# Forgetting attention followed by a gated recurrent block: GpSimd splits one turned chunk of four rows in each head

## The chip, the cores and the metric

One NeuronCore of a Trainium2 chip runs the whole two-layer trunk in one launch. The metric is the device time of the launch in microseconds; lower is better. "SyncE" is the engine that only issues transfers.

## The reference, cut to what matters

x is (1, 2048, 1024) in float32. Layer 0 is forgetting attention over 16 heads of width 64; layer 1 is a gated linear recurrence (RG-LRU). Each layer ends in `LayerNorm(alpha * x + sublayer(x))`. The change touches only the core of the attention:

```python
for blk in range(S // Q_BLOCK):                      # 16 rows of 128 queries
    s = einsum("bhqd,bhkd->bhqk", q[.., q0:q1], k[.., :q1])
    s = s + cum[.., q0:q1, None] - cum[.., None, :q1]
    p = softmax(where(causal, s, -inf))
    outs.append(einsum("bhqk,bhkd->bhqd", p, v[.., :q1]))
...
return (o * silu(gate)) @ w_out
```

## The kernel before, in words

The kernel has four stages: the projection of the attention (`project`), the attention (`attend`), then the output projection, norm and second projection, and the recurrence (`recur`). Each engine runs its own program and they meet only through semaphores, so an instruction that waits holds up everything behind it on its engine. `attend` takes from about 751 to 1600 us.

To keep float32 accuracy on the fast matmul path, a factor is split in a rounded high part and a low part that is the rest (value minus high part); a product is then made from the parts.

**Work units.** A *row* is 128 queries of one head against all keys up to them; a head has 16 rows (0 to 15), and row i has i+1 blocks of 128 keys, in *chunks* of up to 4 blocks (512 keys): i//4+1 chunks. Two heads make a *pair* (8 pairs), so a pair has 32 rows and 80 chunks. Each pair is 32 *steps*, one for each row, and the engines work on different rows in one step s:

- **TensorE** scores row s, chunk by chunk (L779, L780), turns (transposes) row s-3 chunk by chunk into one of four PSUM buffers (`turn`, L793), and in between weighs the values with a *group* of two rows (`weigh`, L813: the high and the low part of the turned probabilities against the values). The group of rows 2g and 2g+1 is weighed in steps 2g+5 and 2g+6, and its first product comes after the first four scores and turns of its step. So rows 8 and 9 are first needed in step 13, rows 10 and 11 in step 15.
- **VectorE** takes the scores of row s out of PSUM into `probs` with a running minimum (L945 for the last chunk of a row, L948 for the others) and makes the low part of row s-3's chunks out of PSUM (`low`, L956).
- **ScalarE** makes the high part of row s-3's chunks out of PSUM (`high`, L879), then the exponential of row s-1 (L869), and in every odd step moves the finished group out of PSUM (`move`, L894 and L895).
- **GpSimd** runs a loop over the 128 groups: `add_halves(n)` (L738, after ScalarE's move), then `finish(n - 4)`: multiply the gate by the softmax scale (L746, which waits until the gate and the scale are loaded), two multiplications with the attention (L752 to the rounded high part, L753 unrounded), one subtraction for the low part (L755). L755 marks the result as ready.
- **SyncE** stores that result (`store_y`, L693), loads gates two groups ahead (L674) and, once in each head, loads the whole next head (`load_head`, L666 and L667: six pieces of 512 KB, two small ones, and values of 1 MB). All of this stands in one queue in program order. In the loop over n, gate n+2 comes first, then the store of result n, then the head's load, when n+5 is a multiple of 8. So `load_head` stands behind the store of the results n = 3, 11, 19, ..., and the gates n = 6, 14, 22, ... stand directly behind it:

```python
for n in range(ALL):
    if n + 2 < ALL - LAG + 2:
        load_gate(n + 2)
    ...
    store_y(n)
    ...
    ahead = n + LAG + 1
    if ahead % GROUPS == 0 and ahead < ALL:
        load_head(ahead // GROUPS, 1)
    if ahead % GROUPS == GT and ahead // GROUPS + 1 < PAIRS:
        load_head(ahead // GROUPS + 1, 0)
```

Here ALL is 128, LAG 4, GROUPS 16, GT 8 and PAIRS 8: 7 heads are loaded by the first of the two conditions inside the stage, 7 by the second. A turn waits until VectorE has made the low part of the chunk that had the buffer before (L788). A weighing waits until the low parts of both its rows are made (L806).

The functions that the diff touches:

Of the kernel before, what the change touches and what calls it, by code (L numbers as in the profile page):

```python
# [19 lines left out]
P = 128  # L20
BANK = 512
ALU = mybir.AluOpType
ACT = mybir.ActivationFunctionType
# [31 lines left out]
def raw(ap):  # L55

    return ap.bitcast(F32)
# [431 lines left out]
def wait(engine, sem, value):  # L489

    if not isinstance(value, int) or value > 0:
        engine.wait_ge(sem, value)
# [7 lines left out]
def attend(nc, stage, qs, ks, vs, gs, cum, ys):  # L500
# [11 lines left out]
    S = qs.shape[2]  # L512
    D = qs.shape[1]
    QT = S // P
    GT = QT // 2
    GW = 2 * P
    STEPS = 2 * QT
# [20 lines left out]
    def width(s, j):  # L538
        return min(BANK, (s % QT + 1) * P - j * BANK)

    with ExitStack() as ctx:
        a = Alloc(nc, ctx, stage)
        q1, q2, k1, k2, val, probs, ph, pl = ({} for _ in range(8))
# [33 lines left out]
        yh = a.sb("yh", [HEAD_DIM, 2, GW], F32R)  # L577
        yl = a.sb("yl", [HEAD_DIM, 2, GW], F32R)
        rden_rows = a.sb("rden_rows", [2 * HG, 2, P])
        a.sb("free", [P, 5 * P])  # L580
        mask = a.sb("mask", [P, BANK])
        least = a.sb("least", [P, ROWS, PB])
        den = a.sb("den", [P, 2, 2 * HG])
# [24 lines left out]
        turned = a.sem("turned")  # L608
        high_out = a.sem("high_out")
        low_out = a.sem("low_out")  # L610
        weighed = a.sem("weighed")
        rden_ready = a.sem("rden_ready")
        rden_turned = a.sem("rden_turned")
# [5 lines left out]
        scaled = a.sem("scaled")  # L619
        gated = a.sem("gated")  # L620
        y_ready = a.sem("y_ready")
        def sync(sp, behind):

            def head_rows(h):
# [96 lines left out]
        def gpsimd(pool):  # L721
            pa_gpsimd(pool)
            pa["summed"](pool)
            nc.gpsimd.memset(mask[:, :], 0.0).then_inc(const_ready, 1)
            pool.wait_ge(const_ready, 1)
            nc.gpsimd.affine_select(out=mask[:, BANK - P:], in_=mask[:, BANK - P:], compare_op=ALU.is_ge, fill=MASKED,
                                    base=0, pattern=[[-1, P]], channel_multiplier=1).then_inc(const_ready, 1)
            pa["products"](pool)
            pool.wait_ge(const_ready, 2)
            nc.gpsimd.memset(raw(q2[1][HEAD_DIM:HEAD_DIM + 4, :]), 1.0).then_inc(ones_ready[1], 1)  # L730
            pool.wait_ge(ones_ready[1], 1)
            nc.gpsimd.memset(raw(k2[1][HEAD_DIM:HEAD_DIM + 4, :]), 1.0).then_inc(ones_ready[1], 1)
            pool.wait_ge(ones_ready[1], 2)
            pa["stored"](pool, pa["last"] + 1)

            def add_halves(n):
                pool.wait_ge(moved, 2 * n + 2)
                nc.gpsimd.tensor_tensor(att[:, n % AR, :], att[:, n % AR, :], low_sum[:, n % 2, :], ALU.add)\  # L738
                    .then_inc(summed, 1)

            def finish(n):

                b, f = n % 2, n // HG
                pool.wait_ge(gate_loaded[n % 4], 16 * (n // 4 + 1))
                pool.wait_ge(scale_loaded[f % 2], 16 * (f // 2 + 1))
                nc.gpsimd.tensor_tensor(gate[:, n % 4, :], scale[:, f % 2, n % HG, :], gate[:, n % 4, :], ALU.mult)\  # L746
                    .then_inc(scaled, 1)
                wait(pool, y_stored[b], 32 * (n // 2))
                wait(pool, scaled, n + 1)
                wait(pool, summed, n + 1)  # L750
                wait(pool, y_ready, n)
                nc.gpsimd.tensor_tensor(yh[:, b, :], att[:, n % AR, :], gate[:, n % 4, :], ALU.mult).then_inc(gated, 1)  # L752
                nc.gpsimd.tensor_tensor(y[:, :], att[:, n % AR, :], gate[:, n % 4, :], ALU.mult).then_inc(gated, 1)  # L753
                wait(pool, gated, 2 * n + 2)
                nc.gpsimd.tensor_tensor(yl[:, b, :], y[:, :], raw(yh[:, b, :]), ALU.subtract).then_inc(y_ready, 1)  # L755

            for n in range(ALL):
                add_halves(n)
                if n >= LAG:
                    finish(n - LAG)  # L760

        def tensor(pe):
# [20 lines left out]
            def turn(it, s, j):  # L783

                if j == 0:
                    wait(pe, probs_ready, it * STEPS + s + 1)
                c = first[s] + j
                wait(pe, low_out, it * CH + c - TB + 1)  # L788
                if it == 0 and c == 0:
                    pa["out"](pe)  # L790
                for k in range(width(s, j) // P):
                    t0 = (j * PB + k) * P
                    mm = nc.tensor.transpose(tps[c % TB][:, k, :], probs[s % ROWS][:, t0:t0 + P], ident[:, :])  # L793
                mm.then_inc(turned, 1)

            def weigh(it, g, lo, hi):

                hp, gh, b = g // GT, g % GT, g % 2
                KT = 2 * gh + 2
                if lo == 0:  # L800
                    if isinstance(it, int) and it == 0 and hp == 0:
                        if gh % 2 == 0:
                            pe.wait_ge(first_val[gh // 2], 16)
                    elif gh == 0:
                        wait(pe, val_loaded[hp], 16 * (it + hp))
                    wait(pe, low_out, it * CH + first[2 * g + 1] + n_chunks[2 * g + 1])  # L806
                    wait(pe, moved, 2 * (it * GROUPS + g - 1))
                    if g % HG == 0:
                        wait(pe, rden_out, (it * GROUPS + g) // HG)
                for kt in range(lo, hi):  # L810
                    c0 = P if kt == KT - 1 else 0
                    for t in (ph, pl):
                        mm = nc.tensor.matmul(ops[b][:, 0, c0:GW], val[hp][:, kt, :], t[b][:, kt, c0:GW],  # L813
                                              start=(kt == 0 and t is ph), stop=(kt == KT - 1 and t is pl))
                if hi == KT:
                    mm.then_inc(weighed, 1)
                    if g % HG == HG - 2:
                        f = (it * GROUPS + g) // HG
                        wait(pe, rden_ready, f + 1)
                        nc.tensor.transpose(ops[b][0:2 * HG, 1, 0:P], rden[:, f % 2, :], ident[:, :]).then_inc(rden_turned, 1)  # L820
# [36 lines left out]
        def scalar(act, beside):  # L857
# [15 lines left out]
            def high(it, s, j):  # L873
                i, g = s % QT, s // 2
                if j == 0:
                    wait(act, weighed, it * GROUPS + g - 1)
                c, n = first[s] + j, width(s, j) // P
                wait(act, turned, it * CH + c + 1)
                nc.scalar.activation(ph[g % 2][:, j * PB:j * PB + n, i % 2 * P:(i % 2 + 1) * P],  # L879
                                     tps[c % TB][:, 0:n, :], ACT.Copy).then_inc(high_out, 1)  # L880

            def move(it, g):
                n, b = it * GROUPS + g, g % 2
# [36 lines left out]
        def vector(dve, beside):  # L920
# [13 lines left out]
            def take(it, s, j):  # L934

                if j == 0:
                    wait(dve, turned, chunks_before(it, s - ROWS + 1))
                c, w = first[s] + j, width(s, j)
                wait(dve, scored, it * CH + c + 1)
                if j:  # L940
                    wait(dve, scores_out, it * CH + c)
                out, scores, found = probs[s % ROWS][:, j * BANK:j * BANK + w], sps[c % SB][:, 0:w], least[:, s % ROWS, j:j + 1]
                before = least[:, s % ROWS, j - 1:j] if j else None
                if j + 1 == n_chunks[s]:
                    nc.vector.tensor_tensor_reduce(out, scores, mask[:, BANK - w:], 1.0, before if j else 3 * MASKED,  # L945
                                                   ALU.add, ALU.min, found).then_inc(scores_out, 1)
                else:
                    nc.vector.tensor_scalar(out, scores, 1.0, before, ALU.mult, ALU.min, accum_out=found)\  # L948
                        .then_inc(scores_out, 1)
# [32 lines left out]
            def step(it, s, begun):  # L982
                def at(d, run):
                    n = s - d
                    if n >= 0 and n < STEPS:
                        run(it, n)
                    elif n < 0 and begun:
                        run(it - 1, n + STEPS)
# [4 lines left out]
                for k, (second, j) in enumerate(alternate(scores_now, turns, 1)):  # L993
                    if k == 1 and s % 2 == 1:
                        at(2, lambda t, n: invert(t, n // 2))
                    if second:
                        low(t_it, t_s, j)
                    else:
                        take(it, s, j)
# [17 lines left out]
            "weighed": lambda e, n: e.wait_ge(weighed, n),  # L1017
            "turned": lambda e: e.wait_ge(turned, PAIRS * CH),
            "scores_out": lambda e: e.wait_ge(scores_out, PAIRS * CH),
            "low_out": lambda e: e.wait_ge(low_out, PAIRS * CH),  # L1020
            "moved": lambda e: (e.wait_ge(moved, 2 * ALL), e.wait_ge(rden_out, ALL // HG)),
            "stored": lambda e, n: [e.wait_ge(y_stored[b], 32 * ((n - b) // 2 + 1)) for b in range(2)],
            "groups": ALL, "half": GT,
# [958 lines left out]
```

## Time and profile before

| what | value |
|---|---|
| median of 3 runs | 2426.8 us (2424.43 to 2430.43) |
| the profiled execution, its own time | 2428.6 us |
| its span, first to last instruction | 2426.8 us |
| TensorE busy | 2376.5 us (98%) |
| VectorE busy | 1352.7 us (56%) |
| ScalarE busy | 1120.2 us (46%) |
| GpSimd busy | 620.0 us (26%) |
| mean granted TensorE clock | 0.995 |

Shares over the whole span mix four stages; in the attention stage VectorE and ScalarE are far busier than over the span. Busy TensorE is modelled: its matmuls are pipelined, so a busy share near 100% does not mean that it does as much as it can. "PEld" is TensorE's loading of weights, which shows where TensorE waits for an operand. The granted clock is given as a share of 2.4 GHz.

### The profile page before, as it was taken

To read this page: it belongs to the slowest core of one execution; us is meant where nothing else is said; L and a number is where in the kernel's file an instruction comes from. 1 tells how busy PE (TensorE), PEld (TensorE's weight loads), DVE (VectorE), ACT (ScalarE), POOL (GpSimd) and SP (SyncE) were. 2 spreads that over 40 slices of the span, in tenths; PEclk is the share of its full clock that TensorE was granted. 3 is DMA by queue.
4 is the path that set the end of the run, shared out by engine and by line. 5 is a ranking of instruction groups with operands and counts; after the bars stand their busy time and mean duration, and the time that the engine had idled before them with its cause. 6 is when DMAs were issued, how large, how long until landed. Compare 5 with 4: busy or idle time off the path is not lost. (4 is left out here: it accounts for less than half of the span.)

```text
span 2426.8 us, 36554 instructions
## 1 busy us (share of the span) xinstructions
PE 2376.5 (98%) x13453; PEld 2046.2 (84%) x13453; DVE 1352.7 (56%) x2764; ACT 1120.2 (46%) x2036; POOL 620.0 (26%) x719
## 2 busy tenths in 40 slices
PE   9999999999999999999999999989999999999998
PEld 7888889999888888888888888877888888887787
DVE  4232121121015888888888888836544566667633
ACT  2131111011115888888888888822014465657300
POOL 0010000000001455554555554525420000000343
PEclk9999999999999999999999999999999999999999
DMA  6424444332235444565545565266533453447672
GB/s 214 134 73 135 115 120 124 111 118 103 68 97 137 105 110 117 125 135 136 116 110 117 125 137 134 82 208 203 180 122 100 140 161 124 137 135 250 232 250 78
DMA packets 221259, 328.78 MB, mean 135 GB/s; under 512 B 17421, under 2 KB 144717, under 8 KB 215261
## 3 DMA queue, kind: packets, MB, share of 16 engines
q1 hardware_dynamic: 220568, 325.91, 47.3%
q8 instruction: 108, 1.77, 0.3%
q0 software_dynamic: 512, 0.53, 0.1%
q14 instruction: 71, 0.57, 0.1%
HBM read 199.89 MB, written 126.48 MB: 134 GB/s over the span
## 5 line engine op out<-in xcount | busy, mean ns | idle before, releaser
L956 DVE TENSOR_TENSOR at_pl<-at_tps,at_ph 128x512 fp32r<-128x512 f32 (+3 forms) x640 | 370.8, 604 | 15.9 <-ACT at_ph L879 15.9
L879 ACT ACTIVATE at_ph<-at_tps 128x512 fp32r<-128x512 f32 (+3 forms) x640 | 318.7, 537 | 125.6 <-PE at_tps L793 117.7
L355 ACT ACTIVATE pa_stg<-pa_ps 128x512 fp32r<-128x512 f32 (+1 forms) x128 | 76.5, 598 | 632.0 <-PE pa_ps L264 626.1
L793 PE MATMUL at_tps<-ident,at_probs 128*128 128x128 f32 x2176 | 341.1, 275 | 8.4 <-DVE at_pl L956 7.1
L813 PE MATMUL at_ops<-at_ph,at_val 128*128 128x256 f32 (+1 forms) x1152 | 315.5, 296 | 0.2 <-DVE at_pl L956 0.2
L869 ACT ACTIVATE at_probs<-at_probs,at_least 128x128 f32<-128x128 f32 (+15 forms) x256 | 308.1, 1203 | 0.2
L264 PE MATMUL pa_ps<-pa_xh,pa_wh 128*128 128x512 f32 x760 | 296.5, 390 | 0.0
L264 PE MATMUL pa_ps<-pa_xh,pa_wl 128*128 128x512 f32 x760 | 295.8, 389 | 0.0
L264 PE MATMUL pa_ps<-pa_xl,pa_wh 128*128 128x512 f32 x760 | 295.7, 389 | 0.0
L813 PE MATMUL at_ops<-at_pl,at_val 128*128 128x256 f32 (+1 forms) x1152 | 295.3, 282 | 0.0
L779 PE MATMUL at_sps<-at_k,at_q 128*128 128x512 f32 (+3 forms) x640 | 277.6, 434 | 9.8 <-DVE at_probs L948 7.2
L793 PEld LDWEIGHTS at_tps<-ident,at_probs 128*128 128x128 f32 x2176 | 254.8, 141 | 31.8 <-DVE at_pl L956 10.3
L813 PEld LDWEIGHTS at_ops<-at_ph,at_val 128*128 128x128 f32 x1152 | 218.7, 190 | 25.6 <-DVE at_pl L956 15.4
L780 PE MATMUL at_sps<-at_k,at_q 68*128 68x512 f32 (+3 forms) x640 | 234.1, 369 | 0.0
L813 PEld LDWEIGHTS at_ops<-at_pl,at_val 128*128 128x128 f32 x1152 | 219.5, 191 | 8.6
L1543 PE MATMUL re_banks<-re_xh,re_wh 128*128 128x512 f32 x512 | 200.0, 391 | 0.0
L1543 PE MATMUL re_banks<-re_xh,re_wl 128*128 128x512 f32 x512 | 199.4, 389 | 0.0
L1543 PE MATMUL re_banks<-re_xl,re_wh 128*128 128x512 f32 x512 | 199.1, 389 | 0.0
L423 DVE TENSOR_TENSOR pa_stg<-pa_ps,pa_stg 128x512 fp32r<-128x512 f32 x64 | 43.4, 689 | 225.4 <-ACT pa_stg L355 225.4
L264 PEld LDWEIGHTS pa_ps<-pa_xh,pa_wl 128*128 128x128 f32 x760 | 142.7, 188 | 29.8
L264 PEld LDWEIGHTS pa_ps<-pa_xl,pa_wh 128*128 128x128 f32 x760 | 142.7, 188 | 29.3
L264 PEld LDWEIGHTS pa_ps<-pa_xh,pa_wh 128*128 128x128 f32 x760 | 142.7, 188 | 29.2
(194 smaller groups left out, 4638.3 us busy)
## 6 DMA issues: line engine op xcount, KB each, us to landing
at_q<-q_halves SPq DMA_DIRECT2D x45, 512.0 KB
at_k<-k_halves SPq DMA_DIRECT2D x45, 512.0 KB
q_halves<-pa_stg SPq DMA_DIRECT2D x32, 512.0 KB, 4.1
k_halves<-pa_stg SPq DMA_DIRECT2D x32, 512.0 KB, 3.7
v_halves<-pa_stg SPq DMA_DIRECT2D x32, 512.0 KB, 2.8
y_gated<-re_work SPq DMA_DIRECT2D x32, 512.0 KB, 3.2
at_val<-v_halves SPq DMA_DIRECT2D x15, 1024.0 KB, 17.4
pa_wst<-in_attn_w_in SPq DMA_DIRECT2D x14, 1024.0 KB, 7.2
```

The source lines that it names most:

```text
L264: mm = nc.tensor.matmul(out, lhs[p](c), rhs[q](c), start=(c == 0 and k == 0), stop=(c == KC - 1 and k == 2))
L355: nc.scalar.activation(out, source(kind, s), func, scale=scale).then_inc(evac_h, 1)
L423: nc.vector.tensor_tensor(lo, source(kind, s), raw(hi), ALU.subtract).then_inc(evac_l, 1)
L779: nc.tensor.matmul(out, q1[hp][:, i * P:(i + 1) * P], k1[hp][:, keys], start=True, stop=False)
L780: nc.tensor.matmul(out, q2[hp][0:K, i * P:(i + 1) * P], k2[hp][0:K, keys], start=False, stop=True)\
L793: mm = nc.tensor.transpose(tps[c % TB][:, k, :], probs[s % ROWS][:, t0:t0 + P], ident[:, :])
L813: mm = nc.tensor.matmul(ops[b][:, 0, c0:GW], val[hp][:, kt, :], t[b][:, kt, c0:GW], start=(kt == 0 and t is ph), stop=(kt == KT - 1 and t ...
L869: nc.scalar.activation(probs[s % ROWS][:, 0:w], probs[s % ROWS][:, 0:w], ACT.Exp, bias=least[:, s % ROWS, n_chunks[s] - 1:n_chunks[s]], sc ...
L879: nc.scalar.activation(ph[g % 2][:, j * PB:j * PB + n, i % 2 * P:(i % 2 + 1) * P], tps[c % TB][:, 0:n, :], ACT.Copy).then_inc(high_out, 1)
L956: nc.vector.tensor_tensor(pl[g % 2][at], tps[c % TB][:, 0:n, :], raw(ph[g % 2][at]), ALU.subtract)\
L1543: mm = nc.tensor.matmul(psum(t), wt[:, b, k, :], chunk(xt, c)[:, k, :], start=(k == 0 and m == 0), stop=(k == KC - 1 and m == 2))
```

## The change

In rows 8 to 11 of each head, the first chunk (j = 0; all of its 512 keys) is split elsewhere. ScalarE copies the turned chunk to SBUF in full float32 (into the unused last quarter of that row's `probs` buffer) instead of writing the high part. GpSimd makes the high part from this copy with a `tensor_copy`, and the low part with a subtraction; VectorE skips the chunk. The turn that reuses the PSUM buffer waits for ScalarE's copy alone; the weighing waits for GpSimd as well (`split_out`), and so does VectorE before it writes the fourth chunk of the row that comes four rows later. There are 8 such chunks in a pair, 64 in all.

GpSimd's loop runs over steps k instead of groups. In step k it first splits the chunk of row k-3, if that row is one of the four; then, if k is odd, it does `add_halves(n)` and the gate's multiplication for group n-4 (`scale_gate`, n = (k-7)//2); if k is even, the rest of the finishing. There, one multiplication is replaced by a `tensor_copy`.

```diff
+    def on_pool(s, j):
+        i = s % QT
+        return QT // 2 <= i < 3 * QT // 4 and j == 0
...
+        def beside_row(s, j):
+            return j == 0 and s % QT < 3 * PB
+        def copy_of(s, j):
+            if beside_row(s, j):
+                return probs[s % ROWS][:, 3 * BANK:].rearrange("p (k q) -> p k q", q=P)
+            return copied[:, 0:width(s, j) // P, :]
...
-            def finish(n):
-                b, f = n % 2, n // HG
+            def scale_gate(n):
+                f = n // HG
                 pool.wait_ge(gate_loaded[n % 4], 16 * (n // 4 + 1))
                 pool.wait_ge(scale_loaded[f % 2], 16 * (f // 2 + 1))
                 nc.gpsimd.tensor_tensor(gate[:, n % 4, :], scale[:, f % 2, n % HG, :], gate[:, n % 4, :], ALU.mult)\
                     .then_inc(scaled, 1)
+            def finish(n):
+                b = n % 2
                 wait(pool, y_stored[b], 32 * (n // 2))
                 wait(pool, scaled, n + 1)
                 wait(pool, summed, n + 1)
                 wait(pool, y_ready, n)
-                nc.gpsimd.tensor_tensor(yh[:, b, :], att[:, n % AR, :], gate[:, n % 4, :], ALU.mult).then_inc(gated, 1)
                 nc.gpsimd.tensor_tensor(y[:, :], att[:, n % AR, :], gate[:, n % 4, :], ALU.mult).then_inc(gated, 1)
-                wait(pool, gated, 2 * n + 2)
+                pool.wait_ge(gated, 2 * n + 1)
+                nc.gpsimd.tensor_copy(yh[:, b, :], y[:, :]).then_inc(gated, 1)
+                pool.wait_ge(gated, 2 * n + 2)
                 nc.gpsimd.tensor_tensor(yl[:, b, :], y[:, :], raw(yh[:, b, :]), ALU.subtract).then_inc(y_ready, 1)
-            for n in range(ALL):
-                add_halves(n)
-                if n >= LAG:
+            def split(it, s, j):
+                i, g = s % QT, s // 2
+                c, n = first[s] + j, width(s, j) // P
+                at = (slice(None), slice(j * PB, j * PB + n), slice(i % 2 * P, (i % 2 + 1) * P))
+                pool.wait_ge(high_out, it * CH + c + 1)
+                nc.gpsimd.tensor_copy(ph[g % 2][at], copy_of(s, j)).then_inc(split_high, 1)
+                pool.wait_ge(split_high, it * SPLITS + splits_in[c] + 1)
+                nc.gpsimd.tensor_tensor(pl[g % 2][at], copy_of(s, j), raw(ph[g % 2][at]), ALU.subtract)\
+                    .then_inc(split_out, 1)
+            for k in range(PAIRS * STEPS + TURN_LAG + 4):
+                if 0 <= k - TURN_LAG < PAIRS * STEPS:
+                    it, s = divmod(k - TURN_LAG, STEPS)
+                    for j in range(n_chunks[s]):
+                        if on_pool(s, j):
+                            split(it, s, j)
+                n = (k - TURN_LAG - 4) // 2
+                if k % 2 == 1 and n >= 0:
+                    add_halves(n)
+                    if n >= LAG:
+                        scale_gate(n - LAG)
+                elif n >= LAG:
                     finish(n - LAG)
...
                 c = first[s] + j
-                wait(pe, low_out, it * CH + c - TB + 1)
+                past = chunks[c - TB]
+                if on_pool(*past):
+                    wait(pe, high_out, it * CH + c - TB + 1)
+                else:
+                    wait(pe, low_out, lows_before(it, c - TB) + 1)
...
-                    wait(pe, low_out, it * CH + first[2 * g + 1] + n_chunks[2 * g + 1])
+                    c = first[2 * g + 1] + n_chunks[2 * g + 1]
+                    wait(pe, low_out, it * LOWS + c - splits_in[c])
+                    wait(pe, split_out, it * SPLITS + splits_in[c])
...
-                nc.scalar.activation(ph[g % 2][:, j * PB:j * PB + n, i % 2 * P:(i % 2 + 1) * P],
-                                     tps[c % TB][:, 0:n, :], ACT.Copy).then_inc(high_out, 1)
+                if on_pool(s, j):
+                    if not beside_row(s, j):
+                        wait(act, split_out, it * SPLITS + copy_free(s, j))
+                    out = copy_of(s, j)
+                else:
+                    out = ph[g % 2][:, j * PB:j * PB + n, i % 2 * P:(i % 2 + 1) * P]
+                nc.scalar.activation(out, tps[c % TB][:, 0:n, :], ACT.Copy).then_inc(high_out, 1)
...
+                if j == 3 and on_pool(s - ROWS, 0) and beside_row(s - ROWS, 0):
+                    wait(dve, split_out, it * SPLITS + splits_in[first[s - ROWS]] + 1)
...
+                    if second and on_pool(t_s, j):
+                        continue
                     if second:
                         low(t_it, t_s, j)
```

## Rows read from the trace of the kernel before

**Rows 1.** The page's first part: busy time, share of the span and instructions of an engine.

```profile
PE 2376.5 (98%) x13453; PEld 2046.2 (84%) x13453; DVE 1352.7 (56%) x2764; ACT 1120.2 (46%) x2036; POOL 620.0 (26%) x719
```

**Rows 2.** Windows: five steps, 11 to 15, of pair 3's first head, cut at VectorE's first score.

```profile
core 0: us, PE busy (x) PEld busy (x) DVE busy (x) ACT busy (x) POOL busy (x), PEclk, DMA share, GB/s
1086.11:1089.68 3.57, 3.57 (x26) 3.20 (x25) 3.44 (x11) 3.26 (x8) 0.19 (x2) 1.00 1.01 220
1089.68:1093.64 3.96, 3.81 (x27) 3.19 (x26) 3.83 (x12) 3.37 (x6) 0.65 (x1) 1.00 1.00 207
1093.64:1097.87 4.23, 4.23 (x32) 3.89 (x31) 4.11 (x12) 3.60 (x7) 0.00 (x0) 1.00 1.13 225
1097.87:1102.36 4.49, 4.49 (x32) 3.93 (x30) 4.37 (x12) 4.05 (x7) 2.06 (x3) 1.00 0.55 143
1102.36:1107.18 4.82, 4.46 (x34) 3.90 (x32) 4.70 (x13) 3.50 (x7) 4.36 (x7) 1.00 0.24 73
```

**Rows 3.** Waits, 800 to 1500 us: waiter, releaser, us in total, times, longest.

```profile
PEld at_sps L779 <- DVE at_probs L948: 18.4, 56, 0.6
PEld at_ops L813 <- DVE at_pl L956: 13.3, 41, 0.4
```

**Rows 4.** Groups by form, same stretch: VectorE's low part of a full chunk.

```profile
L956 DVE TENSOR_TENSOR at_pl<-at_tps,at_ph 128x512 fp32r<-128x512 f32 x375 | 248.7, 684 | 13.2 <-ACT at_ph L879 13.2
```

**Rows 5.** Timeline of GpSimd in pair 3: start us, us, instruction [idle before, releaser].

```profile
1075.81 0.73 POOL L755 TENSOR_TENSOR at_yl<-at_y,at_yh 64x256 fp32r<-64x256 f32 x1
...
1089.60 0.73 POOL L738 TENSOR_TENSOR at_att<-at_att,at_low_sum 64x256 f32<-64x256 f32 x1 [3.38 <-ACT at_low_sum L895]
1100.17 0.73 POOL L746 TENSOR_TENSOR at_gate<-at_scale,at_gate 64x256 f32<-64x256 f32 x1 [9.84 <-DMA at_gate<-gate_path]
...
1127.77 0.74 POOL L755 TENSOR_TENSOR at_yl<-at_y,at_yh 64x256 fp32r<-64x256 f32 x1
```

**Rows 6.** Timeline of SyncE's queue in the same pair.

```profile
1077.07 0.60 SPq L693 DMA_DIRECT2D y_halves<-at_yl  x1
1077.80 1.14 SPq L666 DMA_DIRECT2D at_q<-q_halves  x2
...
1082.34 0.38 SPq L667 DMA_DIRECT2D at_val<-v_halves  x1
1082.76 12.94 SPq L674 DMA_DIRECT2D at_gate<-gate_path  x1
```

**Rows 7.** Line 746 by itself: what ended the idle time before it, us, times.

```profile
  DMA at_gate<-gate_path: 141.1, 15
```

**Rows 8.** Timeline of ScalarE: its high parts of row 9, three chunks merged.

```profile
1089.54 1.36 ACT L879 ACTIVATE at_ph<-at_tps 128x512 fp32r<-128x512 f32 x3
```

**Rows 9.** Timeline of the weight loads: the first ones of groups 4 and 5.

```profile
1093.82 0.19 PEld L813 LDWEIGHTS at_ops<-at_ph,at_val 128*128 128x128 f32 x1
...
1102.50 0.19 PEld L813 LDWEIGHTS at_ops<-at_ph,at_val 128*128 128x128 f32 x1 [0.30 <-DVE at_pl L956]
```

**Rows 10.** Groups by form, GpSimd, whole span: mean ns of one behind the busy time.

```profile
L746 POOL TENSOR_TENSOR at_gate<-at_scale,at_gate 64x256 f32<-64x256 f32 x124 | 90.6, 730 | 152.0 <-DMA at_gate<-gate_path 141.1 <-DMA at_scale<-inverse_sums 10.9
L755 POOL TENSOR_TENSOR at_yl<-at_y,at_yh 64x256 fp32r<-64x256 f32 x124 | 90.4, 729 | 9.7
L239 POOL TENSOR_TENSOR pa_wl<-pa_wst,pa_wh 128x1024 fp32r<-128x1024 f32 x1 | 2.4, 2364 | 0.1
L237 POOL CAST pa_wh<-pa_wst 128x1024 fp32r<-128x1024 f32 x1 | 1.0, 1038 | 6.2 <-DMA pa_wst<-in_attn_w_in 6.2
```

**Rows 11.** Windows: both long idle times of TensorE after the attention, and what follows.

```profile
1625.75:1631.97 6.22, 0.00 (x1) 0.03 (x1) 0.00 (x0) 0.00 (x0) 0.00 (x0) 0.77 0.59 143
1629.11:1635.94 6.83, 3.97 (x9) 3.13 (x10) 0.00 (x0) 0.00 (x0) 0.00 (x0) 0.50 0.98 313
1635.94:1642.00 6.06, 6.06 (x28) 5.01 (x27) 0.99 (x1) 0.00 (x0) 0.00 (x0) 1.00 1.10 352
2209.90:2215.00 5.10, 0.03 (x2) 0.03 (x1) 5.00 (x7) 3.86 (x6) 0.00 (x0) 0.78 0.46 171
2215.00:2219.60 4.60, 4.60 (x11) 3.63 (x12) 4.60 (x5) 4.58 (x5) 0.00 (x0) 0.50 1.00 313
```

**Rows 12.** The chain that ended last, 1620 to 1700 us: start us, us, what.

```profile
1631.97 8.94 PE re_banks L1490 x30
...
1673.14 10.91 PE re_banks L1490 x48
```

More of the change, by code:

```diff
@@ L539, in width, with lows_before @@
         return min(BANK, (s % QT + 1) * P - j * BANK)
+    def on_pool(s, j):
+        i = s % QT
+        return QT // 2 <= i < 3 * QT // 4 and j == 0
+    chunks = [(s, j) for s in range(STEPS) for j in range(n_chunks[s])]
+    splits_in = [sum(on_pool(*c) for c in chunks[:n]) for n in range(CH + 1)]
+    SPLITS = splits_in[CH]
+    LOWS = CH - SPLITS
+    assert S == 4 * BANK and ROWS == PB
+    def lows_before(it, c):
+        return it * LOWS + c - splits_in[c] if c >= 0 else (it - 1) * LOWS + c + CH - splits_in[c + CH]
     with ExitStack() as ctx:
@@ L579, in attend @@
         rden_rows = a.sb("rden_rows", [2 * HG, 2, P])
-        a.sb("free", [P, 5 * P])
+        copied = a.sb("copied", [P, PB, P])
+        a.sb("free", [P, P])
         mask = a.sb("mask", [P, BANK])
@@ L610, in attend @@
         low_out = a.sem("low_out")
+        split_high = a.sem("split_high")
+        split_out = a.sem("split_out")
         weighed = a.sem("weighed")
@@ L621, in attend, with copy_free @@
         y_ready = a.sem("y_ready")
+        def beside_row(s, j):
[4 more added lines that the diff above has]
+            return copied[:, 0:width(s, j) // P, :]
+        def copy_free(s, j):
+            own = [splits_in[n] for n, c in enumerate(chunks) if on_pool(*c) and not beside_row(*c)]
+            k = own.index(splits_in[first[s] + j])
+            return own[k - 1] + 1 if k else own[-1] + 1 - SPLITS
         def sync(sp, behind):
@@ L1019, in attend @@
             "scores_out": lambda e: e.wait_ge(scores_out, PAIRS * CH),
-            "low_out": lambda e: e.wait_ge(low_out, PAIRS * CH),
+            "low_out": lambda e: (e.wait_ge(low_out, PAIRS * LOWS), e.wait_ge(split_out, PAIRS * SPLITS)),
             "moved": lambda e: (e.wait_ge(moved, 2 * ALL), e.wait_ge(rden_out, ALL // HG)),
```

## The prediction

> **What bounds the kernel now.** I read the page's first part, then windows cut by steps, then the waits, then GpSimd and SyncE in order of time, because the change gives a new duty to an engine that nobody waited for. TensorE shows 98% busy and VectorE 56% over the span [rows 1]. But in the five longest steps of a head VectorE is the full one: 3.44 of 3.57 us, 3.83 of 3.96, 4.11 of 4.23, 4.37 of 4.49 and 4.70 of 4.82, while the weight loads fill only 3.2 to 3.9 us [rows 2]. TensorE waits for VectorE in many short pieces [rows 3]. So relief of VectorE in steps 11 to 14, where the change gives it, is aimed at a real bound.
>
> What the relieved work is made to wait for is the other half. In pair 3 GpSimd finishes a result at 1075.81 + 0.73 = 1076.54 [rows 5]. SyncE stores it, issues the next head from 1077.80 on, and then one gate load, which stands 12.94 us in issue, until 1095.70 [rows 6]. The DMA share is 1.0 and more in the three windows up to 1097.87 [rows 2]: the transfers are the limit. GpSimd waits for that gate from 1090.33 to 1100.17, 9.84 us [rows 5]. That is 23.63 us from finished result to usable gate. The wait comes once for each head loaded inside the stage, 14 times; line 746 has 15 waits of this kind, 141.1 us in all, or 9.4 each [rows 7]. Before the change it costs nothing: behind it stand only GpSimd's own multiplications of an old result, which has several groups of room.
>
> **Part 1: VectorE loses four low parts per head.** One takes 684 ns [rows 4], so four are 2.7 us per head. TensorE can use less: its weight loads leave 16.25 - 14.21 = 2.0 us of idle in these four steps [rows 2], and part of that is its own spacing. Bounds 0 and 2.0; I take 1.2 us per head, nearer the middle than either end, since the waits named for VectorE are 0.3 to 0.4 us each [rows 3]. The turn's wait for ScalarE's copy alone is the means to this gain and is priced with it.
>
> **Part 2: GpSimd's split.** No row shows a copy or a subtraction of 128x512 by GpSimd. Copy: 128x1024 took 1038 ns [rows 10]; half is 0.52, the whole 1.04, and I take 0.57. Subtraction: 64x256 took 729 ns and 128x1024 2364 [rows 10]; half of the large one is 1.18, twice the small one 1.46, the line between them gives 1.27, which I take. Between and around them go two waits of 0.1 us. One split is 2.05 us, bounds 1.9 to 2.7. The Trainium skill (GPSIMD Engine Reference, Engine selection) says that two-input work is about twice as slow there as on VectorE; from the 684 ns row that would be an estimate of 1.37 us for the subtraction, and the sum would be 1.4 us higher. The finishing loses a multiplication of 0.73 and gains a copy of about 0.4: 0.3 us less on each result's way.
>
> **Part 3: whom the split now waits for.** In odd step 11 GpSimd does the split of row 8, `add_halves` (the 1089.60 row) and then `scale_gate`, which is the 1100.17 row. In step 12 comes the split of row 9. The gate's wait therefore stands in front of it. ScalarE's copy of row 9's first chunk is there at about 1090.1 [rows 8], and it lies for ten microseconds. Queued behind the wait: row 9's split, the finishing, the splits of rows 10 and 11. Waiting for row 9's split: TensorE's weighing of group 4, which now starts at 1093.82 [rows 9], and VectorE's fourth chunk of row 13 in the same step. No other cover is left: TensorE is in order, and the scores and turns behind the weighing can't pass it.
>
> **The sum for one head**, from the result at 1076.54 (time 0):
> - gate usable 23.63, its multiplication 0.73, split 2.05: group 4 may be weighed at 26.4 (23.63 + 0.73 + 2.05).
> - Today it is weighed at 1093.82 - 1076.54 = 17.28. Later by 9.1 us.
> - From there to the next such result it is 1128.51 - 1093.82 = 34.69 us today [rows 5, 9]. The next head's load hangs on that result, so the delay does not fade; each head pays again. Taken off: 0.3 for the shorter finishing, and what TensorE makes up after the wait, when VectorE and ScalarE have caught up. That is between 0 and 1.8 us, the idle of its weight loads in steps 13 to 15 (13.54 - 11.72 [rows 2]); I take 0.7, as most of it is spacing.
> - A head becomes 9.1 - 1.0 = 8.1 us longer. The gain of part 1 in steps 11 and 12 is lost in the wait, and that of 13 and 14 is the 0.7.
>
> **The clock.** TensorE's granted clock goes to 0.5 (1.2 GHz) in the two long idle times after the attention, 6.22 and 5.10 us, and is still 0.5 for 3.97 and 4.60 us of work behind them [rows 11]. The new idle time is about 9 us, longer than both, so it should fall 14 times. What it costs: the 30 matmuls after the first idle time took 8.94 us where 48 at full clock took 10.91, which is 6.82 for 30 [rows 12]; 2.1 us lost. Bounds: 0, if the clock stays, and 3.4, half of a 6.83 us stretch. I take 2.1. The Trainium skill (TensorE: Matmul & The Clock Gate, "Loop structure matters more than you think") warns of a loop in which the matmuls wait for a DMA each time round and then run cold; by that rule the term is in the sum, without it the time would be 29 us lower.
>
> Total: 14 x (8.1 + 2.1) = 143 us. The first and the last head of the stage have no such load before their step 11; there part 1 gives 2 x 1.2 = 2.4. Net +140. The profiled execution took 2428.6 us, which gives 2569; it stands 1.8 above the median, so 2567 for the median. Everything before and after the attention is untouched. The four new semaphore waits on other engines are met early: rows 10 and 11 are split after row 9, see below.
>
> **The rivals.**
> 1. *Relief without the wait (faster).* If the gate did not stand in front of row 9's split, the change would give 1.2 us in all 16 heads: 2427 - 19 = 2408; at the upper bound of 2.0 it is 2395. For it: VectorE's windows [rows 2]. Against it: the order in the loop, and the 23.63 us. It would decide only if the gate were usable within 17.28 - 2.78 = 14.5 us after the result, 9 us sooner than it is, and the transfers run at a share of 1.0 until then. The change lets them start 0.3 us sooner, no more.
> 2. *The wait, but no fall of the clock.* 14 x 8.1 - 2.4 = 111: 2538. For it: only that both falls come in another stage, among other work. Against it: both came in shorter idle times than the new one [rows 11].
> 3. *A second wait in each head, for row 11.* After row 9's split GpSimd finishes a result (2.0), splits row 10 (2.05), adds halves and scales (1.4) and splits row 11 (2.05): 7.5 us. Group 5 comes 1102.50 - 1093.82 = 8.68 us after group 4 today [rows 9], and longer at a low clock. With a split at its upper bound of 2.7 it is 8.8, and with any wait for ScalarE's move on top 1 to 2 us late: 14 x 1.5 and 14 x 0.65 for the first split give 2567 + 30 = 2597.
> 4. *Nothing*, because TensorE is 98% busy and the gate is no hindrance: 2427.
>
> **How the numbers follow.** Chances: the forecast 0.79, rival 2 0.10, rival 3 0.07, rival 1 0.03, rival 4 0.01. A measurement of this kernel can tell about 0.3%, 7 us, from no change. Faster 0.03, same 0.01, slower 0.96. Own range of the forecast: all terms low (split 1.9, catch-up 1.8, clock 1.6) is 14 x (10.2 - 1.75) - 2 = +116, 2543; high (split 2.7, catch-up 0, clock 2.9) is 14 x (10.2 + 2.15) - 2 = +171, 2598. The range reaches down to rival 2 and up to rival 3: 2532 to 2602.
>
> **What would show it.** Right: the first weight load of group 4 (and 12) idle for about 9 us behind GpSimd's subtraction, 14 times; line 746's wait as long as now, with row 9's split right behind it; a half of a pair near 62 us where it is 52; stretches of granted clock 0.5 inside the attention, the mean falling from 0.995 to about 0.977; VectorE less busy in steps 11 to 14. Wrong: if GpSimd's wait for the gate shrinks or the split comes ahead of it (rival 1), if the clock stays at 1.0 (rival 2), if group 5 waits for GpSimd too (rival 3). In the first head, steps 11 to 14 should be shorter than before.

## The result, and the profile after

The changed kernel takes 2565.41 us (median; 2564.36 to 2567.02), against 2428.25 us for the kernel before beside it: a ratio of 1.057 (95% interval 1.055 to 1.059). The forecast was 2567, from 2532 to 2602. The profiled execution took 2564.4 us with a span of 2562.5, 135.7 us more than the span before.

Part 1 of the page, the counterpart of [rows 1]:

```profile
PE 2394.1 (93%) x13453; PEld 2067.1 (81%) x13453; DVE 1322.2 (52%) x2700; ACT 1120.2 (44%) x2036; POOL 699.4 (27%) x847
```

VectorE has 64 instructions and 30.5 us of work less, 0.48 us for each low part that is gone: its records overlap, so one of 684 ns ([rows 4]) adds less than that to the busy time. GpSimd has 79.4 us more. TensorE's work hardly changes (17.6 us more, part of it at half the clock); its share falls to 93% because it waits. Windows of steps 11 to 14 of one head, as the first four of [rows 2] and with the same columns:

```profile
1009.54:1012.75 3.21, 3.21 (x24) 2.87 (x24) 2.94 (x10) 2.94 (x7) 1.76 (x2) 1.00 0.99 217
1012.75:1016.44 3.69, 3.69 (x29) 3.38 (x28) 3.33 (x12) 3.59 (x7) 0.73 (x1) 1.00 1.03 215
1016.44:1032.14 15.70, 6.80 (x28) 5.90 (x28) 3.67 (x11) 3.99 (x7) 7.81 (x11) 0.68 0.59 136
1032.14:1036.92 4.78, 4.78 (x35) 4.42 (x34) 3.87 (x11) 3.48 (x6) 3.48 (x5) 0.99 0.00 1
```

Steps 11 and 12 are shorter, as the change means them to be (3.21 and 3.69 us against 3.57 and 3.96). Step 13 takes 15.70 us against 4.23. GpSimd in order of time, in the head where the wait falls at 1076 to 1086 us (L772 adds the halves, L779 scales the gate, L801 and L803 are the split, L789, L791 and L793 the rest of the finishing):

```profile
1062.08 0.72 POOL L793 TENSOR_TENSOR at_yl<-at_y,at_yh 64x256 fp32r<-64x256 f32 x1
...
1076.11 0.73 POOL L772 TENSOR_TENSOR at_att<-at_att,at_low_sum 64x256 f32<-64x256 f32 x1 [1.66 <-ACT at_low_sum L964]
1086.45 0.72 POOL L779 TENSOR_TENSOR at_gate<-at_scale,at_gate 64x256 f32<-64x256 f32 x1 [9.61 <-DMA at_gate<-gate_path]
1087.12 0.60 POOL L801 CAST at_ph<-at_probs 128x512 fp32r<-128x512 f32 x1
1087.80 1.26 POOL L803 TENSOR_TENSOR at_pl<-at_probs,at_ph 128x512 fp32r<-128x512 f32 x1
1089.02 0.72 POOL L789 TENSOR_TENSOR at_y<-at_att,at_gate 64x256 f32<-64x256 f32 x1
1089.81 0.39 POOL L791 CAST at_yh<-at_y 64x256 fp32r<-64x256 f32 x1
1090.28 0.73 POOL L793 TENSOR_TENSOR at_yl<-at_y,at_yh 64x256 fp32r<-64x256 f32 x1
1090.95 0.61 POOL L801 CAST at_ph<-at_probs 128x512 fp32r<-128x512 f32 x1
1091.64 1.28 POOL L803 TENSOR_TENSOR at_pl<-at_probs,at_ph 128x512 fp32r<-128x512 f32 x1
```

and TensorE's weight loads in the same place:

```profile
1079.47 0.19 PEld L838 LDWEIGHTS at_sps<-at_k,at_q 68*128 68x128 f32 x1
1089.13 0.29 PEld L877 LDWEIGHTS at_ops<-at_ph,at_val 128*128 128x128 f32 x1 [9.47 <-issue]
1089.30 0.33 PEld L877 LDWEIGHTS at_ops<-at_pl,at_val 128*128 128x128 f32 x1
```

The wait for the gate is as long as before (9.61 us, 9.84 in [rows 5]), but now a split stands behind it. Its subtraction ends at 1089.06, and TensorE, idle for 9.47 us, goes on at 1089.13. The profile names no releaser and writes "issue"; the times show whose end it was. Line 877's own view has "issue: 253.0, 28", two records for each of 14 waits. SyncE's queue shows the reason, as in [rows 6]: the gate's load stands 13.35 us in issue behind the head's load.

```profile
1064.06 1.15 SPq L700 DMA_DIRECT2D at_q<-q_halves  x2
...
1068.59 0.39 SPq L701 DMA_DIRECT2D at_val<-v_halves  x1
1069.02 13.35 SPq L708 DMA_DIRECT2D at_gate<-gate_path  x1
```

Windows of this wait, of the stretch behind it in which the clock stays low, and of the next 4.35 us:

```profile
1080.09:1089.16 9.07, 0.00 (x1) 0.03 (x1) 0.88 (x4) 0.17 (x1) 2.63 (x4) 0.68 0.78 169
1089.16:1093.65 4.49, 4.49 (x19) 4.30 (x20) 1.76 (x6) 2.80 (x5) 3.68 (x6) 0.50 0.13 31
1093.65:1098.00 4.35, 4.35 (x33) 4.04 (x32) 3.03 (x8) 3.01 (x4) 4.19 (x6) 1.00 0.24 77
```

The granted clock is 0.5 (1.2 GHz) for 4.49 us of work, in which TensorE does 19 matmuls where it does 33 in the next 4.35. The mean clock of the execution is 0.968 (0.995 before).

### The profile page after: what moved, and what is told of

It is laid out like the page before. It is cut to its first block and busy times, and to the rows that moved or that the text cites. A ratio compares the mean times of both kernels' runs of the same rounds, so it can differ in the third digit from the quotient of the medians.

```text
span 2562.5 us, 36634 instructions
## 1 busy us (share of the span) xinstructions
PE 2394.1 (93%) x13453; PEld 2067.1 (81%) x13453; DVE 1322.2 (52%) x2700; ACT 1120.2 (44%) x2036; POOL 699.4 (27%) x847
## 5 line engine op out<-in xcount | busy, mean ns | idle before, releaser
L877 PE MATMUL at_ops<-at_ph,at_val 128*128 128x256 f32 (+1 forms) x1152 | 324.7, 303 | 123.9 <-issue 123.7
L949 ACT ACTIVATE at_ph<-at_tps 128x512 fp32r<-128x512 f32 (+2 forms) x576 | 283.9, 530 | 251.2 <-PE at_tps L855 245.1
L855 PE MATMUL at_tps<-ident,at_probs 128*128 128x128 f32 x2176 | 347.4, 278 | 8.4 <-DVE at_pl L1027 7.1
L877 PEld LDWEIGHTS at_ops<-at_ph,at_val 128*128 128x128 f32 x1152 | 226.4, 197 | 153.2 <-issue 129.4
L1027 DVE TENSOR_TENSOR at_pl<-at_tps,at_ph 128x512 fp32r<-128x512 f32 (+2 forms) x576 | 327.1, 595 | 16.0 <-ACT at_ph L949 16.0
L877 PE MATMUL at_ops<-at_pl,at_val 128*128 128x256 f32 (+1 forms) x1152 | 302.8, 288 | 0.0
L1019 DVE TENSOR_SCALAR_CACHE_REDUCE at_probs<-at_sps,at_least 128x512 f32<-128x512 f32 x192 | 144.0, 750 | 176.0 <-PE at_sps L838 161.9
L877 PEld LDWEIGHTS at_ops<-at_pl,at_val 128*128 128x128 f32 x1152 | 227.4, 197 | 8.6
L772 POOL TENSOR_TENSOR at_att<-at_att,at_low_sum 64x256 f32<-64x256 f32 x128 | 93.4, 729 | 280.9 <-ACT at_low_sum L964 280.9
```

Source lines behind the costliest of these rows:

```text
L949: nc.scalar.activation(out, tps[c % TB][:, 0:n, :], ACT.Copy).then_inc(high_out, 1)
L1027: nc.vector.tensor_tensor(pl[g % 2][at], tps[c % TB][:, 0:n, :], raw(ph[g % 2][at]), ALU.subtract)\
```

## The experiments

Two theories stood against each other from the start. Mine: the cost is the place of row 9's split in GpSimd's queue, behind a gate that lands late because the head's load goes ahead of it. The rival: GpSimd is too slow or too late with a split wherever it stands. "Before" is the kernel before on the same chip.

**1. Take the burst away, keep the change (spread).**

```diff
-                ahead = n + LAG + 1
-                if ahead % GROUPS == 0 and ahead < ALL:
-                    load_head(ahead // GROUPS, 1)
-                if ahead % GROUPS == GT and ahead // GROUPS + 1 < PAIRS:
-                    load_head(ahead // GROUPS + 1, 0)
+                for part in range(4):
+                    ahead = n - part + LAG + 1
+                    if n - part < 0:
+                        continue
+                    if ahead % GROUPS == 0 and ahead < ALL:
+                        load_head(ahead // GROUPS, 1, part)
+                    if ahead % GROUPS == GT and ahead // GROUPS + 1 < PAIRS:
+                        load_head(ahead // GROUPS + 1, 0, part)
```

(`load_head` issues two of its large pieces in each of parts 0, 1 and 2, and the values in part 3.)

> The changed kernel, but each head's load is issued in four portions, behind four results in a row (q1 | k1 | q2, k2 and the forget sums | values), so that no gate and no store stands behind 4 MB. Theory (the gate's wait behind the head's load stands in front of row 9's split): the waits of TensorE on GpSimd go, the clock stays near 0.995, and what is left is the relief of VectorE, 1.2 us a head (0 to 2): 2408, 2395 to 2428. Rival (GpSimd is too slow or too late with its splits, gate or not): TensorE still waits in front of groups 4 and 12 for several us, over 2480. Rival (the relief is worth nothing): 2428.

Measured: 2410.06 us, ratio 0.993 (0.992 to 0.994), clock 0.996. A head takes 51.06 us (mean from the first weight load of group 4 or 12 to that in the next head, in order of time), 51.98 before. The same five steps, here in pair 2:

```profile
977.78:980.98 3.20, 3.20 (x24) 2.86 (x24) 2.93 (x9) 2.92 (x7) 1.75 (x2) 1.00 0.96 204
980.98:984.67 3.69, 3.69 (x29) 3.38 (x28) 3.33 (x11) 3.60 (x7) 3.33 (x5) 1.00 1.10 259
984.67:988.70 4.03, 4.03 (x31) 3.73 (x31) 3.60 (x12) 3.40 (x7) 3.59 (x5) 1.00 0.55 117
988.70:993.12 4.42, 4.42 (x34) 4.05 (x32) 3.85 (x11) 3.98 (x7) 4.24 (x6) 1.00 0.81 225
993.12:997.94 4.82, 4.44 (x34) 3.89 (x32) 4.70 (x13) 3.78 (x7) 0.85 (x2) 1.00 0.56 121
```

GpSimd's waits for the gate between 800 and 1600 us, 121.9 us in 13 waits in the changed kernel, have shrunk to one:

```profile
POOL at_gate L786 <- DMA at_gate<-gate_path: 1.7, 1, 1.7
```

The same splits on the same engine cost TensorE no wait once the gate is early, and the relief shows: 0.37, 0.27, 0.20 and 0.07 us in steps 11 to 14 against [rows 2], 0.9 in all. In step 14 VectorE is busy 3.85 of 4.42 us, so it no longer fills the step, and the step is hardly shorter; what holds it now was not tried. There is little room: row 9's split ends only 0.23 to 0.27 us before group 4 is weighed. The rival theory falls.

**2. The burst taken away from the kernel before (spread_before)**, with the same edit.

> The kernel before, with the head's load in four portions in the same way. Theory: line 746's wait of 9.8 us a head goes and the time does not move, since nobody stood behind that wait: 2428, within 7 us. Rival (the burst of transfers cost the kernel before something too): faster by more than 7 us, and then the spread run's gain over before is not the relief's.

Measured: 2425.45 us, ratio 1.000 (0.999 to 1.001). Here too the wait for the gate has all but gone (`POOL at_gate L753 <- DMA at_gate<-gate_path: 1.4, 1, 1.4` between 800 and 1600 us, against 141.1 us in 15 waits), and the time did not move. So the wait was free before, and the gain of run 1 is the relief's: 2425.45 - 2410.06 = 15.4 us, 1.0 us a head.

**3. The gate's multiplication behind the split of its step (late).**

```diff
             def finish(n):
                 b = n % 2
+                scale_gate(n)
...
                     add_halves(n)
-                    if n >= LAG:
-                        scale_gate(n - LAG)
```

> The changed kernel with the gate's multiplication put back into the even step, behind the split of that step. Row 9's split then no longer stands behind the gate, but rows 10 and 11 do. Theory: group 4 is weighed on time; GpSimd waits for the gate until 23.6 us after the result, multiplies and finishes (2.9), splits row 10 (2.1), adds (0.7), splits row 11 (2.1): group 5 at 31.4 us instead of 25.95, 5.4 later per head, less 0.6 made up, and 2.1 for the clock: 6.9 x 14 = 97, 2523 (2490 to 2545). Rival (only row 9's place in the queue mattered): near 2408.

Measured: 2515.86 us, ratio 1.036 (1.035 to 1.038). Row 9's split is on time, row 10's is not. The waits between 800 and 1600 us have two new rows, which [rows 3] had no counterpart for:

```profile
DVE at_probs L1015 <- POOL at_pl L804: 53.8, 13, 4.8
PE at_sps L836 <- DVE at_least L1015: 50.0, 13, 4.5
```

The wait comes one step sooner than I had it: not the weighing of group 5 is stopped first, but VectorE, which must not write row 14's fourth chunk over row 10's copy before GpSimd has read it. TensorE then waits for a score buffer. It is the wait that the change adds to VectorE.

**4. The two gates ahead of the head's load (gates_ahead).**

```diff
+                early = n % 8 in (4, 5) and n <= 109
-                if n + 2 < ALL - LAG + 2:
+                if n + 2 < ALL - LAG + 2 and not early:
                     load_gate(n + 2)
...
                 ahead = n + LAG + 1
+                if n % 8 == 3 and n <= 107:
+                    load_gate(n + 3)
+                    load_gate(n + 4)
```

> The changed kernel with the two gates that stood behind each head's load issued ahead of it; nothing else. Row 9's split no longer stands behind a gate. Theory (the burst hits everything that SyncE issues behind it, the stores of results too): the finishing in step 12 waits until the store of the result two before has landed, some 24 us after the result behind which the head is loaded, finishes (1.9), splits row 10 (2.1), adds and scales (1.4), splits row 11 (2.1): group 5 is weighed at about 31 us instead of 25.95, as in the late run: 2515 (2495 to 2530). Rival (the gate alone was the trouble): near 2410.

Measured: 2527.33 us, ratio 1.042 (1.040 to 1.043). The gate costs nothing now; the finishing waits for the landing of an older result's store, which stands behind the same burst. As in run 3, VectorE is stopped first, by row 10's split (58.5 us in 13 waits between 800 and 1600 us); the forecast named group 5 and was 12 us short. GpSimd's groups:

```profile
L793 POOL TENSOR_TENSOR at_y<-at_att,at_gate 64x256 f32<-64x256 f32 x124 | 91.2, 736 | 125.2 <-DMA y_halves<-at_yl 112.8
L783 POOL TENSOR_TENSOR at_gate<-at_scale,at_gate 64x256 f32<-64x256 f32 x124 | 90.5, 730 | 2.7 <-DMA at_gate<-gate_path 2.7
```

**5. Row 8 alone (row8)**: `return i == QT // 2 and j == 0` in `on_pool`. Its split stands ahead of the gate's wait.

> The changed kernel with row 8 alone split by GpSimd; its split stands ahead of the gate's wait in GpSimd's queue, those of rows 9 to 11 go back to VectorE. Theory (the cost is the place behind the gate, not GpSimd's split as such): no wait of TensorE on GpSimd, the clock at 0.995, and a part of the relief, 0.3 us a head: 2422, 2415 to 2428. Rival (a split by GpSimd delays the weighing wherever it stands): over 2440.

Measured: 2420.64 us, ratio 0.997 (0.996 to 0.998). The gate's wait is still there (124.3 us in 13 waits between 800 and 1500 us) and costs nothing. The clock stays at 0.995.

**6. One part alone: the finishing (finish_alone)**, the kernel before with L752 replaced by a copy of `y`.

> The kernel before with one part of the change alone: in the finishing, one multiplication replaced by a copy. Theory: each result is ready 0.3 us sooner and nobody waits for it, 2428 within 7 us. Rival (the finishing's length matters to the head's load or to the end of the stage): faster by more than 7 us.

Measured: 2425.80 us, ratio 0.999 (0.998 to 1.000). Same, as expected.

**7. The clock: keep TensorE at work while it waits (fill, fill80).** In `weigh`, ahead of its waits:

```diff
+                if lo == 0 and gh == 4 and 0 < it * GROUPS + g - 4 < 116:
+                    for _ in range(60):
+                        nc.tensor.transpose(ops[b][:, 1, P:2 * P], ident[:, :], ident[:, :])
```

> The changed kernel with 60 transposes of the identity into an unused corner of the output bank, put ahead of the 14 weighings that wait for GpSimd; nobody reads them. 60 take about 6.9 us at full clock, less than the 8.4 to 9.5 us that TensorE is idle there, so they cost nothing by themselves. Theory with the clock's term (2.1 us each): no stretch at 0.5 in these places, 14 x 2.1 = 29 us less, 2536. Rival (the clock costs nothing, TensorE is not what limits after the wait): 2565. Rival (the filling delays what it stands in front of): above 2565.

Measured: 2562.57 us, ratio 1.055 (1.053 to 1.057), clock 0.987. By its time this is a miss, and taken alone it would speak for the rival at 2565. But the transposes left 1.8 to 3.3 us of idle time, and the clock fell behind 11 of 14 waits all the same, mostly for a shorter stretch, but with 3.4 us or more of it in work. How much idle time was left does not tell the cases apart: it was 2.8 us in one place without a fall and 2.0 us in one with a fall. The execution still separates heads with and without a fall. Windows from one release to the next; of the four shown the first and the third have the clock at 1.00 throughout, the second and the fourth a fall:

```profile
840.42:900.60 60.18, 57.09 (x422) 51.81 (x423) 43.35 (x118) 43.83 (x90) 33.55 (x49) 1.00 0.47 106
900.60:962.99 62.39, 58.67 (x422) 53.26 (x422) 43.45 (x118) 43.94 (x90) 33.54 (x49) 0.97 0.44 103
...
1085.67:1146.32 60.65, 57.14 (x422) 51.87 (x423) 43.36 (x118) 43.95 (x90) 33.50 (x49) 1.00 0.47 106
1146.32:1207.96 61.64, 58.68 (x422) 53.30 (x423) 43.45 (x118) 43.93 (x90) 33.53 (x49) 0.97 0.45 104
```

So I ran it with `range(80)`.

> As the fill run, with 80 transposes instead of 60: about 9 us, which leaves TensorE no idle time of 2 to 3 us behind them. With 60 the clock still fell behind 11 of the 14 waits, though the heads without a fall were about 2.0 us shorter. Theory (a fall of the clock costs about 2 us a head): no falls, 14 x 2.0 = 28 us less than the changed kernel, 2537, up to 7 us more where 80 transposes outlast the wait. Rival (the clock's fall costs nothing): 2565 or more.

Measured: 2543.39 us, ratio 1.048 (1.047 to 1.050), clock 0.996, with no fall in any of the 14 places (at most about 1 us of idle time is left in front of them). That is 22 us less than the changed kernel, 1.6 us for each fall, with 1120 more instructions on the engine that limits. A head takes 59.76 and 59.98 us in this run's first two windows:

```profile
841.82:901.58 59.76, 59.01 (x441) 53.93 (x442) 43.36 (x118) 43.84 (x90) 33.55 (x49) 1.00 0.46 107
901.58:961.56 59.98, 59.27 (x445) 53.99 (x444) 43.34 (x118) 43.81 (x90) 33.46 (x49) 1.00 0.46 107
```

**8. More relief on top of run 1 (rows46, rows411)**: `on_pool` with `i in (4, 6)` added, and with `QT // 4 <= i`.

> The spread run's kernel with rows 4 and 6 split by GpSimd too (6 chunks a head). VectorE fills steps 7 and 9 as well (2.17 of 2.31 us and 2.95 of 2.96 in the spread run), where these rows are turned. Theory (VectorE bounds these steps, GpSimd has room): 0.3 us in each step, 0.6 a head, 2410 - 10 = 2400. Rival (GpSimd is now late, 7.4 us of work in steps 11 and 12 come on top): TensorE waits for it, 2410 or more.

Measured: 2405.37 us, ratio 0.991 (0.990 to 0.993). A head takes 50.5 us. It is the fastest kernel of the study, 4.7 us below run 1, half of what I had for it; the intervals of the two ratios overlap at 0.992 to 0.993, so it is the heads in the two traces that show the gain, and not the ratios. The heads are 0.5 us shorter, near the 0.6 forecast; see under what stays open.

> The spread run's kernel with all of rows 4 to 11 split by GpSimd (8 chunks a head). Theory (GpSimd's own time now bounds): in the rows46 run it is busy 14.4 of 15.4 us in steps 11 to 14; two more splits of 2 us each in steps 8 and 10 make it about 3 us late for row 9's split, and TensorE waits for it in each head, too briefly for the clock: 2405 + 16 x 3 = 2450 (2420 to 2480). Rival (there is still room): steps 8 and 10 get 0.3 us shorter each, 2396.

Measured: 2452.31 us, ratio 1.011 (1.009 to 1.012). A head takes 53.66 us, 3.1 more than with rows 4 and 6. With eight splits a head GpSimd is too slow, and TensorE waits for it; between 800 and 1600 us:

```profile
PEld at_ops L884 <- issue: 46.2, 26, 2.0
PE at_ops L884 <- issue: 35.9, 25, 1.6
```

The size was right, the place wrong. I had TensorE waiting for row 9's split, but in front of group 4 it is idle for only 0.2 to 0.4 us. It waits twice a head, for the splits of rows 5 and 7, in front of groups 2 and 3. In one head the second split, of row 5, ends at 1034.85 and group 2 starts at 1034.91; group 3 waits 1.65 us in the same way:

```profile
1033.58 1.27 POOL L810 TENSOR_TENSOR at_pl<-at_probs,at_ph 128x512 fp32r<-128x512 f32 x1
1034.91 0.19 PEld L884 LDWEIGHTS at_ops<-at_ph,at_val 128*128 128x128 f32 x1 [2.01 <-issue]
```

GpSimd is busy 15.71 of the 16.40 us from 1029.60, where the first split of the head begins. So its own time bounds these steps, as the theory says, but it does so earlier in the head.

## Why the prediction was right

**The bound.** VectorE fills the steps that the change relieves: shown by the spread run against its control, 1.0 us a head; I had 1.2 between bounds of 0 and 2.0. The 2.7 us of VectorE's work that I named for four low parts are about 2.0 in busy time (0.48 us each).

**The split.** L801 takes 0.60 us and L803 1.26 to 1.30, where I had 0.57 and 1.27 from the line between two sizes. The Trainium skill's factor of about two (GPSIMD Engine Reference, Engine selection) had given an estimate of 1.37; the measured mean of 1.297 us is 1.9 times the 684 ns of VectorE, so the trace agrees, and the line between the rows was nearer.

**The wait, for one head.** From the result at 1062.80 the gate is usable after 23.65 us (forecast 23.63), group 4 is weighed after 26.33 (26.4), and the next such result comes 36.06 later (34.69 - 1.0 + 2.1 = 35.8). It happens 14 times, and since each head's load hangs on that result, it does not fade: thirteen heads from the first release to the last take 806.8 us, 62.06 each, against 51.98.

**The balance of the spans.** The first release is 6.4 us later than the same weighing before, 13 heads add 13 x 10.08 = 131.1, and the rest behind the last release is 1.8 shorter: 135.7. My sum was 140. The head was right within 0.1 us (10.2 against 10.08); I charged 14 of them in full and too little relief at the edges, where two heads' worth comes off the first release. These edges are known less well than the heads: in three executions with heads of 51.98 us (before, runs 2 and 6) the first weighing of a fourth group lies at 779.9 to 781.8 us, and what follows the fifteenth takes 914.7 to 917.3.

**The clock.** I had 2.1 us for a fall, from 30 matmuls in another stage. The fill run's heads give 62.35 (mean of ten with a fall) less 60.33 (three without) = 2.0. The heads of fill80, none with a fall, take 60.34, and those of the changed kernel 62.06: 1.7. The whole times of these two kernels give 1.6; the transposes outlasted the wait in one place of 14, by 0.1 us, so that did not hide more. The clock fell to 0.5 behind every one of the 14 waits of the changed kernel. The Trainium skill (TensorE: Matmul & The Clock Gate, "Loop structure matters more than you think") has the matmuls of a loop run cold behind a long wait for a DMA. Here TensorE waits for GpSimd, which waits for the DMA, and the trace agrees: the clock is low behind all 14. Without the fall a head is 60.3 - 52.0 = 8.3 us longer, where the forecast had 8.1.

The mean clock fell further than my sign for it said (about 0.977): to 0.968. The low stretches are longer than the 6.83 us of [rows 11], 10.24 us in 13 of the 14 places. But only 3.0 to 6.3 us of each lie in work; the rest lies in the wait and costs nothing.

**Luck in the number.** The terms are less exact than the 1.6 us between forecast and median. The wait was put 0.2 us a head too low and the fall 0.1 to 0.5 too high, and over 14 heads these errors partly cancel.

**The rivals.** Relief without the wait (2408) is what the spread run made, at 2410: the mechanism was right and missed only its condition. No fall of the clock: fell. A second wait for row 11 did not appear: its split ends 1.9 to 3.2 us before group 5 is weighed. What I had not weighed is how close VectorE's new wait is; in the changed kernel it hides behind TensorE's, and in runs 3 and 4 it comes first.

**Open.** Of the rows46 run's gain in the heads (7.9 us from the first to the last weighing of a fourth group, against the spread run) 5.6 are left in the span: the first such weighing comes 0.5 us later, and what follows the last one takes 1.7 us longer. What holds the end back was not tried.

## What to carry to other kernels

Before an engine gets work that others wait for, list what it waits for itself, harmless waits above all: a wait of 9.8 us that cost nothing became 8 us a head, and 10 with the clock, once a 2 us job stood behind it. Where the late operand comes behind a burst of transfers, cut the burst (+5.7% became -0.7% here); moving one transfer ahead of it, or one call behind another, hands the wait to the next in the queue (+4.2% and +3.6%). And where TensorE waits for several microseconds, add the work at half clock that follows.

## What the runs showed of the hardware

- Idle time of 1.8 to 3.3 us behind 60 small transposes still let the clock fall in 11 of 14 places, after which 3 to 6 us of work ran at 1.2 GHz. With 80 transposes, and at most about 1 us of idle time, it never fell. I had thought that most of the idle time filled would be enough.
- GpSimd's 128x512 copy with rounding takes 0.60 us, its subtraction 1.3 us. VectorE's work beside them lengthens them little: the subtraction takes 1.26 us with VectorE idle in the wait and 1297 ns on average.
- A transfer of 64 KB issued behind 4 MB stands 13 us in SyncE's issue, and the stores behind it are not issued until it has left.
